# Constant multiplications in TensorE's waits, short matmuls spread over products, and another order at the start of the expert stage

## The reference

```python
h = rmsnorm(x, norm1_w[l]) * (1.0 + scale1) + shift1
proj = h @ w_in[l]                       # 22 chunks of weights
...                                      # mLSTM and differential attention, head by head
x = x + gate1 * (merged @ w_out[l])
h2 = rmsnorm(x, norm2_w[l]) * (1.0 + scale2) + shift2
x = x + gate2 * hierarchical_moe(h2, ...)

# hierarchical_moe: 4 groups of 8 experts
pg_top, g_idx = lax.top_k(softmax(hf @ w_rg + b_rg), 1)     # one group for each token
pe_top, j_idx = lax.top_k(softmax(e_sel), 2)                # two experts of that group
act = silu(hf @ w_gate[e]) * (hf @ w_up[e])
y = y + combine[:, e:e + 1] * (act @ w_down[e])
```

## Time and profile before

| | us |
|---|---|
| median of 3 runs | 1982.66 |
| lowest, highest | 1981.46, 1983.67 |
| the profiled execution | 1981.84 |
| its span, first to last instruction | 1980.1 |

### The profile page before, as it was taken

How to read it: one execution, slowest core, us unless ns; L and a number is a source line. 1 busy time by engine, 2 the same in 40 slices (tenths; PEclk the granted TensorE clock), 3 DMA queues, 4 the chain that set the end, 5 groups by cost and what they waited for, 6 DMA issues and landing times. The chain is left out here.

```text
span 1980.1 us, 34173 instructions
## 1 busy us (share of the span) xinstructions
PE 1918.3 (97%) x14056; PEld 1679.6 (85%) x14056; DVE 1376.7 (70%) x1960; ACT 1092.5 (55%) x1645; POOL 81.7 (4%) x93
## 2 busy tenths in 40 slices
PE   7999998999999999999889999998999989999999
PEld 5888987999888888889879988887988988888888
DVE  5675875676666666676656666656776669999997
ACT  5444672554544554457455554444655457787785
POOL 1000006000000000000230000000000000000000
PEclk9999999999999999999999999998899989999999
DMA  9765330443665556544115466653332329999995
GB/s 386 280 234 186 135 126 25 150 170 131 242 255 210 204 206 247 209 171 148 65 49 198 142 224 228 237 191 115 128 127 108 135 98 353 356 373 377 374 379 190
DMA packets 56645, 404.01 MB, mean 204 GB/s; under 512 B 6376, under 2 KB 6560, under 8 KB 8240
## 3 DMA queue, kind: packets, MB, share of 16 engines
q1 hardware_dynamic: 51504, 370.73, 50.6%
q0 software_dynamic: 4992, 31.15, 4.1%
HBM read 400.80 MB, written 1.06 MB: 203 GB/s over the span
## 5 line engine op out<-in xcount | busy, mean ns | idle before, releaser
L306 DVE TENSOR_TENSOR weights_split<-ring,weights_split 128x1024 fp32r<-128x1024 f32 x696 | 819.5, 1221 | 205.8 <-ACT weights_split L296 201.8
L296 ACT CAST weights_split<-ring 128x1024 fp32r<-128x1024 f32 x696 | 693.5, 1048 | 218.4 <-PE ps L323 203.4
L321 PE MATMUL ps<-weights_split,act 128*128 128x512 f32 (+1 forms) x896 | 334.4, 373 | 12.7 <-DVE weights_split L306 12.6
L323 PE MATMUL ps<-weights_split,act 128*128 128x512 f32 (+1 forms) x896 | 329.5, 368 | 0.0
L322 PE MATMUL ps<-weights_split,act 128*128 128x512 f32 (+1 forms) x896 | 328.9, 367 | 0.0
L321 PEld LDWEIGHTS ps<-weights_split,act 128*128 128x128 f32 x896 | 169.1, 189 | 40.8 <-DVE weights_split L306 12.6
L323 PEld LDWEIGHTS ps<-weights_split,act 128*128 128x128 f32 x896 | 168.9, 188 | 28.5
L322 PEld LDWEIGHTS ps<-weights_split,act 128*128 128x128 f32 x896 | 169.2, 189 | 26.4
L321 PE MATMUL ps<-act,weights_split 128*128 128x256 f32 x608 | 174.6, 287 | 0.3
L322 PE MATMUL ps<-act,weights_split 128*128 128x256 f32 x608 | 169.7, 279 | 0.0
L323 PE MATMUL ps<-act,weights_split 128*128 128x256 f32 x608 | 169.7, 279 | 0.0
(11 more groups left out here) (545 smaller groups left out, 3366.7 us busy)
## 6 DMA issues: line engine op xcount, KB each, us to landing
ring<-stream SPq DMA_DIRECT2D x348, 1024.0 KB, 4.8
stretch<-ada_in POOLq DMA_DIRECT2D x24, 1024.0 KB, 5.3
y<-c_in POOLq DMA_DIRECT2D x4, 512.0 KB, 5.8
act_room<-mem_in SPq DMA_DIRECT2D x2, 1024.0 KB, 4.9
consts<-w_consts SPq DMA_DIRECT2D x1, 1376.0 KB, 11.6
x<-x_in SPq DMA_DIRECT2D x1, 1024.0 KB, 4.9
stretch<-mem_in POOLq DMA_DIRECT2D x1, 1024.0 KB, 9.6
bias_t<-bias_scratch POOLq DMA_DIRECT2D x1, 1024.0 KB, 12.4
```

The source lines that it names most:

```text
L296: core.nc.scalar.copy(self.hi[:, self.place(i), part], core.slot(chunk)[:, part]).then_inc(self.rounded.sem, 1)
L306: core.nc.vector.tensor_tensor(self.lo[:, self.place(i), part], core.slot(chunk)[:, part], self.hi[:, self.place(i), part].bitcast(F32), A ...
L321: nc.tensor.matmul(out, lhs[0], rhs[0], start=start, stop=False, **kw)
L323: return nc.tensor.matmul(out, lhs[1], rhs[0], start=False, stop=stop, **kw)
```

## The change

In `second_stage`, PE multiplies constants (`keep_busy(core, bank, n)`: n matmuls of the ones matrix by the identity, 128 x 128 float32, results never read) at three places: 7 at the stage's start, 13 behind the sums of the squares, 4 behind the spread. The three bursts of small matmuls are taken apart: those of L2966 stand one by one behind each feature block of chunk 6 (both halves), those of L2972 behind the feature blocks 0, 2, 4 and 6 of the first half of chunk 7, those of `head_spreads(0)` in the same way in chunk 20.

In `expert_stage`, PE multiplies 12 constants ahead of the ranks and 12 behind them. ACT rounds the tokens ahead of chunk 0. DVE makes `token_lo` ahead of the selection, and subtracts chunk 0 behind it; it splits the near slots and subtracts chunk 1 ahead of the router's part, not behind it. PE gathers feature block by feature block, high and low parts together, and `gate_up(0, ...)` waits feature block by feature block for `near_split`.

```diff
+def keep_busy(core, bank, n):
+    for _ in range(n):
+        core.nc.tensor.matmul(core.ps[:, bank, 0:P], core.const("ones"), core.const("ident"), start=True, stop=True)
...
@@ expert_stage, PE
+                    if u == 0:
+                        pe.wait_ge(near_split.sem, near_split.at(max(ch + 1, 2)))
...
+            keep_busy(core, 2, 12)
             pe.wait_ge(route_loaded.sem, route_loaded.at(16))
             pe.wait_ge(grouped.sem, grouped.at(1))
...
             ins.then_inc(ranked.sem, 1)
+            keep_busy(core, 2, 12)
             pe.wait_ge(chosen.sem, chosen.at(1))
-            pe.wait_ge(tokens_rounded.sem, tokens_rounded.at(4))
-            gather_near(token_hi, True)
             pe.wait_ge(tokens_ready.sem, tokens_ready.at(4))
-            gather_near(token_lo, False)
+            for k in range(KB):
+                gather_near(k)
             turn_selection()
-            pe.wait_ge(near_split.sem, near_split.at(KB))
@@ expert_stage, ACT
-            weights.round(act, 0)
             act.wait_ge(inverted.sem, inverted.at(1))
...
+            weights.round(act, 0)
             act.wait_ge(shifted.sem, shifted.at(1))
@@ second_stage, PE
+                        if c == QK_SUMS:
+                            head_square(m, k)
+                        elif c == GATE_SPREAD and m == 0 and k % 2 == 0:
+                            gate_part(k // 2)
+                        elif c == HEAD_SPREAD and m == 0 and k % 2 == 0:
+                            head_part(k // 2, k == 6)
...
+            keep_busy(core, E0, 7)
             pe.wait_ge(weighted.sem, weighted.at(2))
...
             ins.then_inc(summed.sem, 1)
+            keep_busy(core, E0, 13)
...
                 ins.then_inc(spread.sem, 1)
+            keep_busy(core, E0, 4)
             for c in range(BR_M):
```

More of the change, by code:

```diff
@@ L1967, in turn_selection, with gather_near @@
                 ins.then_inc(back_turned.sem, 1)
-            def gather_near(part, first):
-                for k in range(KB):
+            def gather_near(k):
+                for part in (token_hi, token_lo):
                     for t in range(TT):
                         ins = nc.tensor.matmul(near_bank(k), part[:, t, k * P:(k + 1) * P], select[:, t, 0:2 * SLOTS],
[L1973 to L1976, removed]
+                                               start=part is token_hi and k % 2 == 0 and t == 0,
+                                               stop=part is token_lo and t == TT - 1, skip_group_check=True)
+                if k % 2:
+                    ins.then_inc(near_filled.sem, 1)
             def gather_far(k):
@@ L2151, in _ @@
             dve.wait_ge(grouped.sem, grouped.at(1))
-            weights.subtract(dve, 0)
+            for t in range(TT):
+                for half in range(2):
+                    dve.wait_ge(tokens_rounded.sem, tokens_rounded.at(2 * t + half + 1))
+                    part = slice(half * 512, (half + 1) * 512)
+                    nc.vector.scalar_tensor_tensor(token_lo[:, t, part], raw_tokens(t, half), rs[:, t:t + 1],
+                                                   token_hi[:, t, part].bitcast(F32), ALU.mult,
+                                                   ALU.subtract).then_inc(tokens_ready.sem, 1)
             dve.wait_ge(route_loaded.sem, route_loaded.at(16))
@@ L2167, in _ @@
             ins.then_inc(chosen.sem, 1)
[L2168 to L2173, removed]
-                                                   ALU.subtract).then_inc(tokens_ready.sem, 1)
+            weights.subtract(dve, 0)
+            for k in range(KB):
+                dve.wait_ge(near_rounded.sem, near_rounded.at(k // 2 * 2 + 2))
+                split_slots(a_lo[:, 0:2, k, :], near_bank(k), a_hi[:, 0:2, k, :], k, near_split)
+            weights.subtract(dve, 1)
             v(nc.vector.tensor_tensor(counts[:, :], counts[:, :], first_chunk, ALU.mult))
@@ L2187, in _ @@
             v(first_max(ex[:, :, 2, :], ex[:, :, 0, :], st[:, :, 1:2], E, ex[:, :, 3, :]))
-            for k in range(KB):
-                dve.wait_ge(near_rounded.sem, near_rounded.at(k // 2 * 2 + 2))
-                split_slots(a_lo[:, 0:2, k, :], near_bank(k), a_hi[:, 0:2, k, :], k, near_split)
-            weights.subtract(dve, 1)
             v(nc.vector.scalar_tensor_tensor(ex[:, :, 4, :], ex[:, :, 2, :], NEG, ex[:, :, 0, :], ALU.mult, ALU.add))
@@ L2640, in second_stage @@
     SCORE, TURN, VALUE, E0, E1 = 2, 4, 5, 6, 7
+    QK_SUMS, GATE_SPREAD, HEAD_SPREAD = 6, 7, 20
     pairs_of = [(0, 4), (1, 5), (2, 6), (3, 7)]
@@ L2806, in product_chunk, with head_square, gate_part @@
                         ins = products(nc, ps[:, c % 2, m * S:(m + 1) * S], lhs, mov, k == 0, k == KB - 1)
-                ins.then_inc(core.used, 1)
+                        if c == QK_SUMS:
[4 more added lines that the diff above has]
+                            head_part(k // 2, k == 6)
+                ins.then_inc(core.used, 1)
+            def head_square(t, i):
+                if t == 0 and i == 0:
+                    pe.wait_ge(qk_squared.sem, qk_squared.at(1))
+                at = 16 * t + 8 * (i // 4) + i % 4
+                ins = nc.tensor.matmul(ps[:, E0, at:at + 5:4], h[:, i, t * P:(t + 1) * P], core.const("head_ones")[:, 0:P:64],
+                                       start=True, stop=True)
+                if t == TT - 1 and i == KB - 1:
+                    ins.then_inc(qk_summed.sem, 1)
+            def gate_part(i):
+                if i == 0:
+                    pe.wait_ge(step.sem, step.at(5))
+                ins = nc.tensor.matmul(ps[:, SCORE + i // 2, (i % 2) * S:(i % 2 + 1) * S],
+                                       core.const("row_pick")[0:4, i * P:(i + 1) * P], a, start=True, stop=True)
+                if i == 3:
+                    ins.then_inc(gate_spread.sem, 1)
             def branch_unit(c, j):
@@ L2908, in head_turns, with head_part @@
                 ins.then_inc(head_turned.sem, 1)
+            def head_part(i, last):
+                if i == 0:
+                    pe.wait_ge(head_moved.sem, head_moved.at(1))
+                ins = nc.tensor.matmul(ps[:, E0 + i // 2, i % 2 * S:(i % 2 + 1) * S],
+                                       core.const("row_pick")[0:4, i * P:(i + 1) * P], head_rows[:, :], start=True, stop=True)
+                if last:
+                    ins.then_inc(head_spread.sem, 1)
             def head_spreads(which):
@@ L3016, in _ @@
                     head_turns(0)
-                elif c == 19:
-                    head_spreads(0)
             branch_unit(BR_M, 0)
```

14 lines of the change are left out of this document (removed).

## The result

The changed kernel takes 1986.15 us (median of 20 runs, 1981.09 to 1989.87), the kernel before, in the same series, 1982.82 us (20 runs, 1978.63 to 1987.14). The ratio is 1.0014, with a 95% interval of 1.0008 to 1.0021: the change costs 2.8 us (1.6 to 4.2). That is under the 0.2% I had set as the limit, but a series of this length tells it from nothing. I had forecast no change, 1982.4 us, and my range holds the measured time; but the time moved clearly, and to the slower side.

What follows compares the result with a forecast made beforehand. TensorE, busy 97% of the span, was taken as the bound, with time winnable where it waits or runs at 1.2 GHz. Terms +1.8 - 3.3 - 0.5 - 0.5 - 0.6 + 3.3 = +0.2 gave 1982.0, forecast 1982.4 us; range 1977.5 to 1987.0.

Steps and rivals of the forecast that it cites:

- Chunk 6: Second stage: 48 products with 16 small matmuls between take 9.1 us instead of 12.4, -3.3 us if the clock holds.
- chunk 7's: Second stage: burst taken apart costs +1.2 us in borders but avoids half clock; net -0.5 us, bounds -0.5 and +1.2.
- Chunk 20: Second stage: head-scale spread taken apart; same -0.5 us as for chunk 7, its low stretch having the same length.
- Start of the second stage: Clock may fall in the squares' sums, so the 13 constants run slowly and delay the spread: +1.8 us, bounds 0 to +3.4.
- for the order: Expert stage: faster gather, first unit ends earlier, but TensorE then waits for VectorE's shares; gain only 0.6 us.
- for the fall: Expert stage: new pause plus 20 small matmuls lower the clock near 1630 us; +3.3 us, bounds 0 to +6.1.
- The wait was moved: Expert stage: TensorE finishes the first unit at 1624.7 and waits until 1627.5 for the shares, a new 2.8 us pause.
- That the clock holds everywhere: Rival, whole kernel: second stage's start even and the expert pause free; -4.9 us, 1977 us; chance 0.15.
- That small matmuls between products keep the clock low: Rival, chunks 6, 7 and 20: chunk 6 takes 17.1 us, +4.7; full price 1993 us; chance 0.08.
- That the constants don't hold the clock in the gather: Rival, expert stage: gather stays slow, shares up to 2.6 us late; about 1984.5 us; chance 0.12.

Runs made afterwards that it cites:

- The fill: Changed kernel plus 12 unread matmuls before TensorE's wait for the shares: 1980.17 us, ratio 0.9995 to the kernel before; on another chip 1984.16 us, 1.0006.
- order-only profile: Kernel before with the expert stage's new order alone, without its 12 and 12 constants: 1984.94 us, ratio 1.0016; profile of its longest execution, 1990.5 us.

## Why the prediction was wrong, and where it was right

**Chunks 6, 7 and 20 (forecast -3.3 - 0.5 - 0.5 = -4.3 us).** Chunk 6 is right: with its sums it takes 9.2 us (1408.75 to 1417.98) for the 9.1 of the working, and B is 3.2 us less with chunk 6 alone apart (48.36) than with the bursts together (mean of five profiles 51.6). The working read the fall there as coming after 4.9 us of small matmuls; it came at 1407.1, 2.1 us into the burst, and the rest of the 4.9 us was at half clock already. That changes nothing in the term. **The step that failed is chunk 7's.** I gave its term two bounds, -0.5 and +1.2, and took -0.5 because this one trace had a fall near 1421. In the four other profiles with the bursts together there was no fall in chunk 7, its burst ran at full clock (8 matmuls in 1.99 us) and B was 50.0 to 51.6 us for the 53.11 of the execution that I read. Taken apart, the burst costs +1.4 instead of the -0.5. So one low stretch of one execution was taken for the kernel's.

Chunk 20 is the other way round: a low stretch of 3.4 to 6.8 us near its burst (1529 to 1534 us) is in all six profiles with that burst together and in none of the eight with it apart, and the mean of C falls from 182.3 to 181.1 us, though the ranges overlap (179.96 to 184.88 and 179.58 to 182.77). Since the low stretch of 3.4 us near chunk 7 falls now in B and now in C, the two together say most: 233.9 us is the mean of the five profiles with all bursts together, 230.8 of the eight with all three apart, 230.7 with chunk 6's alone. The gain is 3.1 us and not 4.3; what chunk 20 brings, chunk 7 takes. C holds something that the working had no term for: the second spread of head scales, left as one burst of the same form near 1554 to 1563 us. A low stretch of 3.4 us begins 0.2 to 1.5 us behind it in four of the eight profiles with chunk 20's burst apart and in none of the six with it together. Whether the change moved the fall there or these are chance, so few profiles don't tell. No run has chunk 7's or chunk 20's burst apart alone.

**Start of the second stage (forecast +1.8, bounds 0 to +3.4).** Right: +1.72 in the two profiles, +1.8 between the means of five and eight. In all five profiles with the seven constants the clock fell inside the sums, 2.3 to 3.4 us behind their start, and half of the 13 or more ran at 1.2 GHz. The constants do shorten the low stretch there, to 3.4 or 6.8 us from 10.2 or 13.7 without them; but before the first product TensorE isn't the engine waited for, and a late spread is all that counts.

**The expert stage (forecast -0.6 for the order, +3.3 for the fall, bounds 0 to +6.1).** Right in mechanism and size. The wait was moved: 2.60 us of idle time in front of the shares for the 2.8 of the working, releaser L2210. The fall came behind it. D + E rose by 2.99, 3.01 and 2.94 us in the three profiles with the whole change, where I had +2.7: in the changed kernel -0.27 for the shares' earlier start, where I had -0.6, and +3.26 for the fall, where I had +3.3. The fill removed the fall in three profiles of four. But the model for it, a pause of 2.7 us with a fall at its end at 1608.5, was again one execution's: in the five other profiles without constants ahead of the ranks the clock fell 0.2 to 1.8 us ahead of that pause, while TensorE still had small matmuls. That the fall behind the shares came as forecast is therefore in part luck; its being tied to the wait rests on the fill and on the order-only profile, where it began inside the wait.

**The sum.** With the measured terms it is +1.8 - 3.1 + 3.0 = +1.7 us instead of +0.2; measured +2.8 (1.6 to 4.2) and, on another chip, +3.6 (1.8 to 5.4). The sum lies just inside the first interval and just outside the second; about 1 us or more isn't accounted for. In the profile of the changed kernel there were 2.0 us more ahead of the second stage, with low clock near 332 and 950 us, where nothing was changed; the kernels without the change show such stretches as well in several profiles (near 949 us with the bursts apart, near 331 us with chunk 6 alone), so I put them to the spread of executions. The first square of the second stage comes between 1345.9 and 1352.4 us in the fourteen profiles, which are all of one program up to there. Whether the change makes the stretches likelier stays open. The forecast had a small slip of its own: its sum was +0.2 us on the profiled execution, but I added only half of that execution's distance to the median, so the forecast stood 0.3 us under the median before.

**The rivals.** That the clock holds everywhere fell with the stretch from 1629 us. That small matmuls between products keep the clock low fell in all nine profiles with chunk 6's sums spread: none had a low clock there. That the constants don't hold the clock in the gather fell too: in all eight profiles with them the gather ran at 1.00, and in all six without them most of it ran at 0.50. But they can do something I had not listed: in an execution whose clock is low already at the stage's start they hold up the ranks (1.3 us of VectorE's wait, and D 26.56 instead of 23.77, which has a second fall in it).

## What to carry to other kernels

Ask of every stretch of low clock whether TensorE is the engine waited for: here some 20 us of half clock were removed, much of it from places where it waits for VectorE and ScalarE, and the time didn't fall. Before an engine is made faster into a wait, look for the wait that comes next; when the other engine's list stays as long, the idle time only moves, and it may bring a fall of the clock into work that had none. And don't cost an edit by a low stretch that one execution shows: look for its cause in the rows, and keep the bound without it as the likelier.

## What the runs showed of the hardware

- With a burst of 32 matmuls of 2 columns between chunks 5 and 6 the clock fell in all five profiles, 2.1 to 4.4 us behind the burst's start, busy as TensorE was; one by one between triples of 256-column products the same matmuls left it at 1.00 in all nine. The small one costs 0.22 us there.
- Matmuls on 4 rows with 256 columns cost 0.24 us each in a burst (8 in 1.92 from start to start) and 0.31 in pairs between products, and the product behind each pair takes 0.23 us to its successor instead of 0.12; with three apart B is 1.4 us longer than with chunk 6's alone.
- Where the instructions are the same, low stretches still differ from execution to execution: at the burst of head sums 3.4 us in one profile and 6.8 in four, at the second stage's start without constants 10.2 us in one and 13.7 in seven, with all of them 3.4 in two and 6.8 in three, and one of 3.4 us near chunk 7 came in one profile and later, or not at all, in the others. The runs of one kernel in one series spread over 5 to 13 us.
- Constants meant to hold the clock take nearly twice as long if it is already low: 24 instructions took 2.92 us in one execution and 5.46 in another.
